# Small tables regrouped or padded, so that the operands of split matrix products start at other addresses

## The reference, cut to what matters

```python
# first block, twice (l = 0, 1): attention as in the source, then
h = rmsnorm(x, norm_mlp);  x = x + square(relu(h @ w_up)) @ w_down          # 1024 -> 4096 -> 1024
# second block, layer 0: input projection of the even mixer, layer 1: of the odd mixer
h = x @ w_in                                                               # w_in_even, w_in_odd
# second block, both layers: gate and embedding beside the routed experts
ple = sigmoid(x @ ple_gate_w[i] + ple_gate_b[i]) * (p[i] @ ple_w[i])
```

## The kernel before

| product | activations, start mod 2048 | weights, start mod 2048 | weights less activations | small tensors between or below |
|---|---|---|---|---|
| `in` | `h` 768 | `in_w` 1280 | 512 | six tables of 2560 bytes in all |
| `wy` | `h`, `mixed` 768 | `wy_w` 768 | 0 | none |
| `mlp` | `h2`, `u` 768 | `mlp_w` 800 | 32 | `n2_tables`, 32 bytes |
| `ei` | `xT_e` 1120 | `ei_w` 1152 | 32 | `nf_gain`, 32; below `xT_e` also `mla_g`, `add2`, `back2`, `gb`, `tot`, `dec` |
| `oi` | `xT_o` 1024 | `oi_w` 1216 | 192 | `gqa_g` 32, `add3` 32, `on_rk` 128 |
| `pl` | `xT`, `pT` 1920 | `pl_w` 192 | 320 | `lg`, `aff`, `mx`, `top` and others |
| `w_o`, layer 0 and 1 | `mixT` 1280, 768 | `w_o_w` 1536, 1024 | 256 | 256 bytes of statistics |

## Time and profile before

### The profile page before, as it was taken

How to read it: one execution, slowest core, us unless ns; L and a number is a source line. 1 busy time by engine, 2 the same in 40 slices (tenths; PEclk the granted TensorE clock), 3 DMA queues, 4 the chain that set the end, 5 groups by cost and what they waited for, 6 DMA issues and landing times. The chain is left out here.

```text
span 3446.9 us, 39641 instructions
## 1 busy us (share of the span) xinstructions
PE 3242.4 (94%) x15918; PEld 2176.3 (63%) x15918; DVE 1296.3 (38%) x1781; ACT 958.9 (28%) x1570; POOL 238.9 (7%) x377
## 2 busy tenths in 40 slices
PE   7999999999999999999997999999988999999996
PEld 5885578887787567888785466444436556544442
DVE  4315554242522564333366472111116656111112
ACT  3325433132322533323242431000004543000001
POOL 1004200000101410000000200000000320000000
PEclk9999999999999999999997999999999999999999
DMA  5410122321540022222311216999992112799997
GB/s 156 129 43 24 64 87 94 98 93 57 137 127 32 1 86 86 98 92 92 89 36 23 86 56 257 422 424 424 424 417 75 61 62 93 304 423 424 424 424 303
DMA packets 234149, 590.12 MB, mean 171 GB/s; under 512 B 42690, under 2 KB 146184, under 8 KB 184852
## 3 DMA queue, kind: packets, MB, share of 16 engines
q1 hardware_dynamic: 234004, 588.08, 45.1%
HBM read 581.75 MB, written 2.10 MB: 169 GB/s over the span
## 5 line engine op out<-in xcount | busy, mean ns | idle before, releaser
L2579 PE MATMUL ps<-w_ring,xe 128*64 128x512 f32 x1024 | 235.9, 604 | 5.0 <-PEq L119 5.0
L422 DVE TENSOR_TENSOR mlp_w_lo<-w_ring,mlp_w_hi 128x2048 fp32r<-128x2048 f32 x62 | 142.1, 2292 | 212.7 <-ACT mlp_w_hi L382 212.7
L357 PE MATMUL ps<-h_hi,in_w_hi 128*128 128x512 f32 (+1 forms) x528 | 207.0, 392 | 2.1 <-DVE h_lo L430 2.1
L357 PE MATMUL ps<-h_hi,in_w_lo 128*128 128x512 f32 (+1 forms) x528 | 205.6, 389 | 0.0
L357 PE MATMUL ps<-h_lo,in_w_hi 128*128 128x512 f32 (+1 forms) x528 | 205.6, 389 | 0.0
L357 PE MATMUL ps<-h_hi,mlp_w_hi 128*128 128x512 f32 x512 | 202.6, 396 | 2.1 <-DVE h_lo L430 2.1
L357 PE MATMUL ps<-h_hi,mlp_w_lo 128*128 128x512 f32 x512 | 202.5, 396 | 0.0
L357 PE MATMUL ps<-h_lo,mlp_w_hi 128*128 128x512 f32 x512 | 202.5, 395 | 0.0
L357 PE MATMUL ps<-mlp_w_hi,u_lo 128*128 128x512 f32 x512 | 202.3, 395 | 0.0
L357 PE MATMUL ps<-mlp_w_hi,u_hi 128*128 128x512 f32 x512 | 202.2, 395 | 0.0
L357 PE MATMUL ps<-mlp_w_lo,u_hi 128*128 128x512 f32 x512 | 202.2, 395 | 0.0
(11 more groups left out here) (560 smaller groups left out, 6480.5 us busy)
## 6 DMA issues: line engine op xcount, KB each, us to landing
w_ring<-in_w SPq DMA_DIRECT2D x192, 1024.0 KB, 12.4
ex_front<-in_w SPq DMA_DIRECT2D x96, 1024.0 KB, 12.8
ex_back<-in_w SPq DMA_DIRECT2D x96, 1024.0 KB, 13.0
w_ring<-in_w_in SPq DMA_DIRECT2D x32, 1024.0 KB, 5.4
w_ring<-in_w_up SPq DMA_DIRECT2D x32, 1024.0 KB, 5.5
w_ring<-in_w_down SPq DMA_DIRECT2D x32, 1024.0 KB, 5.0
w_ring<-in_cmp_w SPq DMA_DIRECT2D x16, 512.0 KB, 5.0
w_ring<-in_w_out SPq DMA_DIRECT2D x8, 1024.0 KB, 6.0
```

Source lines behind the costliest of these rows:

```text
L357: mm = pe.matmul(ps[0:o.rows, bank[k], 0:o.cols], lhsT, rhs, start=(o.first and j == 0), stop=(o.final and j == len(o.mm) - 1))
L422: dve.tensor_tensor(w.lo[:, home(n), 0:used], ring.slots[:, n % RING, 0:used], w.hi[:, home(n), 0:used].bitcast(F32), ALU.subtract).then_i ...
L2579: mm = pe.matmul(ps[rows, bank + half, :], lhsT, slot(2 * m + a)[:, kk, 512 * half:512 * half + 512], start=(k == 0), stop=(k == DC - 1))
```

## The change

It changes shapes and places of small tables, and no instruction that computes.

- `mlp`: `n2_tables` grows from 8 columns to 512 (32 to 2048 bytes); the gain still uses the first 8.
- even mixer: `mla_g`, `add2`, `gb`, `tot`, `dec` and `nf_gain` become parts of one tensor `e_small` of 512 bytes, which lies where `mla_g` lay.
- odd mixer: `gqa_g`, `add3` and `on_rk` become parts of one tensor `o_small` of 2048 bytes, which lies where `gqa_g` lay.
- `pl`, both layers: an unused tensor `rw_gap` of 192 bytes is allocated ahead of `pl_w`.

```diff
-        gain = ctx.enter_context(sbuf(nc, "n2_tables", [P, DC], F32))
-        gemm(nc, "mlp", ps, ring, tiles, 2, nxt, rms_flips(C, I["norm_mlp"][l], h, ring, gain[:, :]), side=tail)
+        gain = ctx.enter_context(sbuf(nc, "n2_tables", [P, BANK], F32))
+        gemm(nc, "mlp", ps, ring, tiles, 2, nxt, rms_flips(C, I["norm_mlp"][l], h, ring, gain[:, 0:DC]), side=tail)
...
-    gw, gb, reset = sb("gw", [2 * GRANK, 2, 256]), sb("gb", [P, 2, 2]), sb("la_reset", [P, T])
+    gw, gb, reset = sb("gw", [2 * GRANK, 2, 256]), small[:, 32:36].rearrange("p (d c) -> p d c", d=2), sb("la_reset", [P, T])
...
-    tot, dec = sb("tot", [P, 2, 2, T // GC]), sb("dec", [P, 2, 2, T // GC])
+    tot, dec = (small[:, c:c + 32].rearrange("p (c d n) -> p c d n", c=2, d=2) for c in (64, 96))
...
-            gains, add, back = sb("mla_g", [P, 3], c2), sb("add2", [P, 3, 2], c2), sb("back2", [2, 3, P], c2)
+            small, back = sb("e_small", [P, P], c2), sb("back2", [2, 3, P], c2)
+            gains, add, gain = small[:, 0:3], small[:, 8:14].rearrange("p (n m) -> p n m", m=2), small[:, 16:16 + DC]
...
-                gain = sb("nf_gain", [P, DC], c3)
...
-    gains, ones, back = sb("gqa_g", [P, 2]), sb("add3", [P, 4]), sb("back3", [8, 4, P])
+    small, back = sb("o_small", [P, BANK]), sb("back3", [8, 4, P])
+    gains, ones, rk = small[:, 0:2], small[:, 4:8], small[:, 32:64].rearrange("p (i h) -> p i h", i=TT)
...
-    rk, rs = sb("on_rk", [P, TT, 8]), pair(nc, ctx, "on_rs", [8, T])
+    rs = pair(nc, ctx, "on_rs", [8, T])
...
     rws = pair(nc, ctx, f"rws{i}", [P, DC, NE])
+    sb("rw_gap", [P, 48])
```

More of the change, by code:

```diff
@@ L1437, in _, with even_beside @@
                     pe.matmul(ps[:, 1 + n % 7, :], back_r[:, n, :], rs.lo[:, :], start=False, stop=True).then_inc(s.spread, 1)
-def even_beside(nc, ctx, ps, C, I, x, ring, n_split, cq, ckv, cs, gq, gk, lr, og, gains, add, back):
+def even_beside(nc, ctx, ps, C, I, x, ring, n_split, cq, ckv, cs, gq, gk, lr, og, small, gains, add, back):
     def sb(name, shape, dt=F32):
@@ L1924, in even_mixer @@
             gv, gr, lr = sb("gv", [P, TT, 512], c2), sb("gr", [P, TT, 512], c2), sb("lr", [2 * GRANK, T], c2)
-            side = even_beside(nc, c2, ps, C, I, x, ring, lambda n: 4 + n, cq, ckv, cs, gq, gk, lr, og, gains, add, back)
+            side = even_beside(nc, c2, ps, C, I, x, ring, lambda n: 4 + n, cq, ckv, cs, gq, gk, lr, og, small, gains, add, back)
             with ExitStack() as c3:
@@ L1945, in even_mixer @@
                 tiles += [tokens(E[n] + 256 * m, dst[:, :, 256 * m:256 * m + 256]) for n, dst in (("gv", gv), ("gr", gr)) for m in range(2)]
-                gain = sb("nf_gain", [P, DC], c3)
                 with nc.allow_non_contiguous_dma("narrow columns"):
-                    gemm(nc, "ei", ps, ring, tiles, 2, lead=rms_flips(C, I["norm_final"], h, ring, gain[:, :]), also=tables,
+                    gemm(nc, "ei", ps, ring, tiles, 2, lead=rms_flips(C, I["norm_final"], h, ring, gain), also=tables,
                          side=side, banks=4)
```

## The result

| | before, us | after, us |
|---|---|---|
| median of the runs | 3447.98 (4 runs, 3446.20 to 3449.67) | 3423.66 (4 runs, 3421.50 to 3428.11) |
| profiled execution, its span and its own time | | 3423.4, 3425.14 |
| ratio after / before | | 0.9935, 95% interval 0.992 to 0.995 |

A later timing of the unaltered kernel (last experiment) gave a ratio of 0.994 (0.9927 to 0.9953).

A forecast was written before the change was run, and what follows sets the result against it. The prediction took TensorE, busy for 94% of the span, to bound the kernel. Its terms, 20.3 + 1.3 - 1.5 + 0.6 - 0.3 + 1.2 = 21.6 us less, took 3448.4 to 3426.8 us, range 3421.5 to 3432.

The forecast's parts named there:

- `mlp`, 20.3 us: Two layers of 1536 matmuls go from 233.3 to 226.7 ns each, 20.3 us gained.
- the mechanism: Byte distance between weights and activations sets 512-column matmul spacing: 0 or 512 fast, 32 slow; chance 0.76.
- Alignment by itself: Rival: each operand's start on a multiple of 256 decides; `pl` stays at 229.1 ns, 3428.0 us; chance 0.16.
- The addresses do nothing: Rival: `mlp` is slower for something of its own, so the time stays 3448.4 us; chance 0.05.
- The distance without its sign: Distances of 192 and 320 bytes, in `oi` and `pl`, lie between fast and slow, at 229.0 and 229.1 ns.
- A lower clock in `mlp`: Rival: denser matmuls lower the granted clock in `mlp`; at 0.95 the time is 3464 us; chance 0.03.
- `ei`, net +0.2: In `ei`, 192 matmuls of 512 columns gain 1.3 us, 384 of 256 columns lose 1.5 us.
- The 121: Spacing in ns taken for 256-column matmuls in `ei` after the change, from `in` at 512; 117 before.
- `oi` and `pl`, -0.3 and -1.2: `oi` gains 0.6 us at 512 columns and loses 0.3 at 256; `pl` gains 1.2 us over two layers.
- Gated linear attention, 0 within 1.3 us: Its moved operands were taken to change nothing, with 1.3 us gain or loss as bound.
- The sum: All terms together: 21.6 us less, a span of 3425.3 us and a median of 3426.8 us.

The follow-up runs named there:

- last experiment: Kernel after, unaltered, timed in five rounds: median 3426.19 us (6 runs) against 3446.05 (11 runs), ratio 0.994.
- `mlp` alone: Kernel before with only `n2_tables` enlarged to 2048 bytes: median 3425.50 us (6 runs) against 3445.67 (17 runs), ratio 0.9947.
- all but `mlp`: Kernel after with the `n2_tables` edit undone, the other three edits kept: median 3447.75 us (12 runs), ratio 1.0004.
- the kernel after once more: Kernel after, unchanged, profiled a second time: 3425.79 us.
- 64 and 128 apart: Kernel after with `n2_tables` at 64 bytes in the first layer and 128 in the second, spacing weights and activations so: 3448.27 us (one run).

## Why the prediction was right, point by point

- **`mlp`, 20.3 us: right to 0.1 us**, and so was the mechanism. The distance of the operands sets the spacing (0 apart off any multiple of 256: 226.7 ns); with this edit alone the medians differ by 20.2 us, without it by nothing measurable.
- **Alignment by itself** falls by the same run, and by `pl`, which reached 227.3 ns in its long stretch (35 matmuls).
- **"The addresses do nothing"** falls too. Between `mlp` alone and all but `mlp`, the 20.3 us go with `n2_tables`. The Trainium skill's sentence in "TensorE: Matmul & The Clock Gate", "Part 2: What happens when you issue a matmul", that loading the next weights steals no read bandwidth from the running matmul, was read in the prediction as a distance that costs nothing. So read, these traces don't agree: 226.7 against 233.3 ns by the distance alone. Whether read bandwidth is what is lost, or what else in the chip makes the distance count, is not shown by any run.
- **The distance without its sign** was the mechanism's one flaw. The prediction put 192 and 320 between the fast and the slow; with the sign, 192 gives 229 ns and 320 gives 233.3.
- **A lower clock in `mlp`**: no. The granted clock is 1.00 in each `mlp` window above, at either spacing.
- **`ei`, net +0.2: came out at -0.37.** Both parts of the mechanism were there. 512 columns go from 233.3 to 226.9 ns (118 matmul steps in 26.77 us); 256 columns from 117.4 to 120.3 ns (311 steps in 37.41 us). The 121 came from the estimate of what is in flight: by its own starts, `in` at 512 has 120.0 ns. Over the stage, the 512 columns gained 1.1 us and the 256 lost 1.1; the remaining 0.3 us is a break of eight transposes, 1.23 us before and 0.91 after, which no term held.
- **`oi` and `pl`, -0.3 and -1.2: mis-sized.** I took the settled spacing for every matmul. Two outputs of 24 matmuls in `oi`, each behind a break, before:

```profile
2627.48 0.48 PE L357 MATMUL ps<-xT_o_hi,oi_w_hi 128*128 128x512 f32 x1
2627.80 0.40 PE L357 MATMUL ps<-xT_o_lo,oi_w_hi 128*128 128x512 f32 x1
...
2629.87 0.39 PE L357 MATMUL ps<-xT_o_lo,oi_w_hi 128*128 128x512 f32 x1
...
2632.84 0.40 PE L357 MATMUL ps<-xT_o_hi,oi_w_lo 128*128 128x512 f32 x1
```

  and after:

```profile
2599.98 0.49 PE L357 MATMUL ps<-xT_o_hi,oi_w_hi 128*128 128x512 f32 x1
2600.31 0.40 PE L357 MATMUL ps<-xT_o_lo,oi_w_hi 128*128 128x512 f32 x1
...
2602.39 0.39 PE L357 MATMUL ps<-xT_o_lo,oi_w_hi 128*128 128x512 f32 x1
...
2605.34 0.39 PE L357 MATMUL ps<-xT_o_hi,oi_w_lo 128*128 128x512 f32 x1
```

  Both take 5.36 us. From the second start on, the first nine steps are 2.07 / 9 = 230 ns before and 2.08 / 9 = 231 ns after; the 13 steps behind them 2.97 / 13 = 228 and 2.95 / 13 = 227. The stream needs some ten matmuls after a break to reach 226.7 ns (11 and 16 at the start of the two `mlp`), and a run of 24 has lost by then what it gains later. `pl` breaks as often: -0.50 in place of -1.2 us. In `oi` at the full clock (the kernel after once more) the stage came out at 80.24, no gain at all: its steps of 512 columns gained 0.28 us where 0.6 was forecast, and its steps of 256 lost 0.28, as forecast (0.3).
- **Gated linear attention, 0 within 1.3 us: the bound was wrong.** It priced a spacing, while the earlier trace rows had a clock of 0.71 in that stretch. The stage's length moved from 63.2 to 54.8 us with that clock, and in `mlp` alone it did so with nothing of it moved.
- **The sum** came out 1.9 us below the predicted span of 3425.3. In that one execution -8.4 us and +5.9 us (`oi`, second attention and `wy`) of clock nearly cancelled; the timed runs, where the clock averages out, give 19.9 to 24.3 us against 21.6. The range held for the right reason: all eleven executions of the unaltered kernel after lie in it, from 3421.50 to 3431.09 us. But its bounds left the largest source of spread out, the clock outside `mlp`, and that the first median came so near was in part luck.

**Open.** Why the gated linear attention has 62.2 to 63.4 us in the three traces with both `mlp` slow, 54.5 to 57.4 in the five with both fast, and 57.3 to 58.0 in the five others, among them 64 and 128 apart, whose `mlp` is nearly as slow as before. Thirteen traces don't tell a tie to the stages ahead from chance. Nor do they tell whether the moved tables make the clock fall more often in `oi`: it takes more than 81 us in five of the eight traces with its tables moved and in one of the five without.

## What to carry to other kernels

Where two stages run the same matmul and differ by a few per cent in spacing, with the clock at 1.00 and nothing waited for, compare where their stationary and moving operands start: here a distance of 0 or 256 modulo 512 bytes gave 226.7 ns for 512 columns and 32 to 128 gave 233.3 (for 256 columns the order was the other way round), and one pad in a long unbroken stream was worth all that the change brought. Don't expect it in short outputs between other work, where the stream doesn't settle. And in a stage whose granted clock is below 1.00, bound the forecast by that clock, not by the instructions.

## What the runs showed of the hardware that was not expected

- Off a multiple of 256 the spacing takes more than one value: 228.9 ns with the stationary operand 192 bytes past the moving one, 233.3 the other way round, and both at 448.
- One operand of three at a bad distance slows all three (231.6 and 233.4 ns on average), unevenly: steps of 232.0, 239.7 and 228.3 ns.
- At the good distance, the stream reaches its spacing only after 10 to 16 matmuls.
- For 256 columns the order is reversed: 120.3 ns at a distance of 0, 117.4 at 32.
- The kernel before, on one core, ranged from 3435.08 to 3454.61 us over 17 runs: 19.5 us, as much as the change moves its median.
